# Expert weights of a mixture-of-experts layer: loads of 4 MB in four buffers instead of 2 MB in eight

## The chip, the core and the metric

The kernel runs on one core of a Trainium2 chip. The metric is the device time of one launch in microseconds. A TensorE matmul reads its weights (stationary operand) and its moving operand from SBUF and writes to PSUM; VectorE (DVE) and ScalarE (ACT) move and combine what it leaves there; the SyncE queue (SP) issues nearly all DMA transfers.

## What is computed

One decoder layer on 256 tokens of 1024 channels in float32: an input projection, a pooling mixer beside a dilated attention, an output projection, and then a mixture of experts, which is nearly all of the weight traffic:

```python
h2 = rmsnorm(x, g_ffn)
logits = h2 @ w_router + b_router            # 32 experts, the best 4 per token
for e in range(N_EXPERTS):
    gu = h2 @ w_gu[e] + b_gu[e]              # [256,1024] @ [1024,2048]
    gate = min(gu[:, :1024], 7);  lin = clip(gu[:, 1024:], -7, 7)
    act = gate * sigmoid(1.702 * gate) * (lin + 1)
    out += combine[:, e:e+1] * (act @ w_down[e] + b_down[e])     # [1024,1024]
return rmsnorm(x + out, g_final)
```

The weights of one expert are 8 MB of w_gu and 4 MB of w_down; all 32 experts are 384 MB (402.65 million bytes). Every expert is loaded, whichever tokens chose it.

## The kernel before

**Front part.** The first 120 us are the projections, the attention and the router. The input weights `win`, their split copies `wsp`, `hTh` and the output weights `wout` lie in the same 128 KB per partition of SBUF that later hold the expert weights (`raw`, line 105). So the first expert loads wait, one buffer after the other, until that part of the memory is free (lines 305 to 316).

**Units and buffers.** `raw` has eight buffers of 16 KB per partition, 2 MB each. A unit is one transfer into one buffer. A unit of w_gu is 256 rows of the matrix, two neighbouring rows to a partition; four units make an expert's w_gu. A unit of w_down is 512 rows, four neighbouring rows to a partition; two units make an expert's w_down. A partition's share is one contiguous run of 16 KB in memory either way (`load`, line 293). Because neighbouring rows lie in one partition, the other operand has to be taken with the same stride: `gather` takes the channels of `h2` with a step of two, `turn_gu` the columns of `gu` with a step of four, and the transposes of the bias (line 995) as well.

**Order.** Experts go in pairs. Up to 64 tokens are gathered for each (`gather`, with a one-hot matrix `disp` as moving operand); `gu_unit` multiplies one row of a w_gu unit per call, 16 matmul records per unit; ScalarE copies the sum from PSUM to `gu`; `turn_gu` transposes it; VectorE adds the bias and clips (`clip`), ScalarE takes the sigmoid, and VectorE forms `actT` (line 769). `down_unit` multiplies a w_down unit by it, 16 matmul records; ScalarE copies the result to `ysc`, and `scatter` multiplies it by the gates and adds it over the tokens. The second expert of a pair is worked on while the first one's activation is made: TensorE's order within `iteration` (line 1071) is w_gu of the pair's second expert (with the scatters of the pair before between its rows), w_down first half of the first expert, gathers for the next pair, `turn_gu`, w_down second half, w_gu of the next pair's first expert, then w_down of the second expert. The loads have the same order. The last pair has no next one.

**Release.** `unit_used` counts the units that TensorE has read. SP waits for the count that frees the buffer (line 335) and issues the next load into it. `raw_loaded[s]` says that buffer s has landed; TensorE waits for it at a unit's first matmul. All eight buffers (16 MB) are filled before the first expert's matmuls; the other 184 units follow one release after the other.

**End.** After the last w_down units come the last scatters, the sums, the final norm and two stores.

Of the kernel before, what the change touches and what calls it, by code (L numbers as in the profile page):

```python
# [42 lines left out]
UW = 2048  # L43
RAW = 8
GU_U, DN_U = 4, 2
EARLY = RAW - GU_U
# [38 lines left out]
def hybrid_layer(nc, x, g_mix, w_in, w_pool, pool_scale, w_out, g_ffn, w_router, b_router,  # L85
                 w_gu, b_gu, w_down, b_down, g_final, consts, out):
    KB = 1024
    with ExitStack() as ctx:
# [15 lines left out]
        W = PAD + T  # L104
        raw = at("raw", [P, RAW, 2, UW], F32, 0)
        acc = at("acc", [P, TT, D], F32, 144 * KB)
# [113 lines left out]
        x_loaded = [sem(f"x_loaded{t}") for t in range(TT)]  # L220
        raw_loaded = [sem(f"raw_loaded{s}") for s in range(RAW)]
        win_loaded = [sem(f"win_loaded{c}") for c in range(DC)]
        const_loaded, vec_loaded, wout_loaded = sem("const_loaded"), sem("vec_loaded"), sem("wout_loaded")
# [58 lines left out]
        def _(sp):  # L282
# [10 lines left out]
            def load(e, first, s):  # L293

                dst = raw[:, s].rearrange("p r n -> p (r n)")
                if first < GU_U:
                    src = w_gu[0, bass.ds(e, 1), 2 * first * P:2 * (first + 1) * P, :].rearrange(
                        "a (p r) n -> p (a r n)", r=2)
                else:
                    u = first - GU_U  # L300
                    src = w_down[0, bass.ds(e, 1), 4 * u * P:4 * (u + 1) * P, :].rearrange(
                        "a (p r) n -> p (a r n)", r=4)
                sp.dma_start(dst, src).then_inc(raw_loaded[s], 16)

            for c in range(PRE_U):
                sp.wait_ge(win_low, 2 * c + 2)
                load(0, c, c)
            sp.wait_ge(win_used, DC)
            load(1, 1, 5)
            load(1, 2, 6)  # L310
            sp.wait_ge(scores, 2)
            load(1, 0, 4)
            sp.wait_ge(probs_turned, 6)
            sp.dma_start(gffn[:], g_ffn.broadcast_to([P, D])).then_inc(gffn_loaded, 16)
            sp.wait_ge(half_projected, 1)
            load(1, 3, 7)
            sp.wait_ge(attended, 2)
# [9 lines left out]
            def iteration(j, half, last):  # L327
                i = j * 2 + half
                a = pair_of(i) * 2
                nxt = pair_of(i + 1) * 2  # L330
                for k in range(EARLY, ITER_U + (0 if last else EARLY)):
                    if last and k in range(GU_U + DN_U, 2 * GU_U + DN_U):
                        continue
                    at_ = k - (GU_U if last and k >= 2 * GU_U + DN_U else 0)
                    sp.wait_ge(unit_used, i * ITER_U + PRE_U + at_ - RAW + 1)
                    s = buffer(half, at_)
                    if k < GU_U + DN_U:
                        load(a, k, s)
                    elif k < 2 * GU_U + DN_U:
                        load(nxt, k - GU_U - DN_U, s)  # L340
                    elif k < ITER_U:
                        load(a + 1, k - GU_U - DN_U, s)
                    else:
                        load(nxt + 1, k - ITER_U, s)
# [56 lines left out]
        def _(act):  # L401
# [124 lines left out]
            def iteration(i, last):  # L526
                gu_copy(i * 2 + 1, 1, used(i, GU_U))
                if not last:
                    gather_copy(0, i * 2 + 3)
                    gather_copy(1, i * 2 + 4)  # L530
                sigmoid(i * 2 + 1)
                y_copy(i, 0, used(i, 6))
                if not last:
                    gu_copy(i * 2 + 2, 0, used(i, 10))
                    sigmoid(i * 2 + 2)
                    y_copy(i, 1, used(i, 12))
                else:
                    act.activation(scrap[:], c_("ones")[:, 0:1], ACT.Sqrt)
                    act.wait_ge(unit_used, used(i, ITER_U - GU_U))
                    act.activation(ysc[0:SLOTS, 1, :], ps[0:SLOTS, Y[1], :], ACT.Copy).then_inc(outputs_ready, 1)  # L540
# [281 lines left out]
        def _(pe):  # L822
# [169 lines left out]
            for m in range(DC):  # L992
                for h in range(2):
                    col = 2 * m + h
                    src = bgu[:, h * FE:(h + 1) * FE].rearrange("e (u q r) -> e u r q", q=P, r=4)[:, m // 4, m % 4, :]
                    ins = pe.transpose(ps[:, 2, col * E:(col + 1) * E], src, c_("ident", E)[:, 0:E])
# [13 lines left out]
            def gather(job):  # L1010

                for c in range(4 * job, 4 * job + 4):
                    for t in range(TT):
                        ins = mm(ps[:, M[job], (c % 4) * P:(c % 4 + 1) * P],
                                 h2[:, t, :].rearrange("p (k q r) -> p k r q", q=P, r=2)[:, c // 2, c % 2, :],
                                 disp[:, t, :, :], start=t == 0, stop=t == TT - 1)
                ins.then_inc(gathered, 1)

            def gu_unit(half, c, s, value):
                r = c % 2  # L1020
                if r == 0:
                    pe.wait_ge(raw_loaded[s], value)
                for b in range(2):
                    for h in range(2):
                        col = h * FE + b * 512
                        ins = mm(ps[h * SLOTS:(h + 1) * SLOTS, GU[half] + b, :], xT[:, c, half, :],
                                 raw[:, s, r, col:col + 512], start=c == 0, stop=c == DC - 1)
                if r == 1:
                    ins.then_inc(unit_used, 1)

            def down_unit(half, u, s, value):
                pe.wait_ge(raw_loaded[s], value)
                for r in range(4):
                    m = 4 * u + r
                    for h in range(2):
                        col = r % 2 * D + h * 512
                        ins = mm(ps[h * SLOTS:(h + 1) * SLOTS, Y[half], :], actT[:, half, m, :],
                                 raw[:, s, r // 2, col:col + 512], start=m == 0, stop=m == DC - 1)
                ins.then_inc(unit_used, 1)

            def turn_gu(e):

                pe.wait_ge(gu_copied, e + 1)
                for m in range(DC):
                    ins = pe.transpose(ps[:, M[m // 4], (m % 4) * P:(m % 4 + 1) * P],  # L1045
                                       gu[:].rearrange("p (u q r) -> p u r q", q=P, r=4)[:, m // 4, m % 4, :], c_("ident"))
                ins.then_inc(gu_turned, 1)
# [12 lines left out]
            for c in range(DC):  # L1060
                pe.wait_ge(xT_ready, c // 4 + 1)
                gu_unit(0, c, c // 2, 16)
            pe.wait_ge(bdown_loaded, 32)
# [7 lines left out]
            def iteration(j, half, last):  # L1071
                i = j * 2 + half
                for k in range(DC):
                    gu_unit(1, k, *unit(j, half, k // 2))
                    if k == 1:
# [17 lines left out]
                pe.wait_ge(act_ready, i * 2 + 1)  # L1093
                down_unit(0, 0, *unit(j, half, 4))
                if not last:
# [9 lines left out]
                turn_gu(i * 2 + 1)  # L1105
                down_unit(0, 1, *unit(j, half, 5))

                gap = GU_U if last else 0
                if not last:
                    for k in range(DC):  # L1110
                        gu_unit(0, k, *unit(j, half, 6 + k // 2))

                pe.wait_ge(act_ready, i * 2 + 2)
                for u in range(DN_U):
                    down_unit(1, u, *unit(j, half, 10 + u - gap))
                    if u == 0 and not last:
# [43 lines left out]
```

## Time and profile before

| | us |
|---|---|
| median of 3 runs | 1057.15 (1057.02 to 1059.78) |
| the profiled execution | 1058.68 |
| its span | 1056.9 |
| TensorE busy in it | 966.2 (91%) |
| VectorE, ScalarE busy | 248.6, 141.8 |
| transfers | 419.96 MB, mean 397 GB/s |

The page cuts the span into 40 slices of 26.4 us. A digit is the busy share in tenths, and PEclk the granted TensorE clock in tenths of full speed. The chain of waits is followed back from the last instruction, each step to what released it. In lists of instructions, x is the count, and the bracket is the idle time before and what ended it. MB and GB in the views are of 10^6 and 10^9 bytes, KB of 1024.

### The profile page before, as it was taken

What the parts mean: (1) busy time and instruction counts of PE and PEld (TensorE: products, weight loads), DVE (VectorE), ACT (ScalarE), POOL (GpSimd) and SP (SyncE); (2) the same over time, 40 slices, a digit from 0 to 9 for tenths busy, and PEclk for the clock granted to TensorE, in tenths of its full rate; (3) what the DMA queues carried; (4) which work ended last, traced back from release to release, by engine and by line L of the source; (5) the groups of instructions that cost most, each with busy time, mean ns of one, the idle gap of its engine ahead of it and who ended that gap; (6) DMA issues with size and microseconds to landing.
All of it is one profiled execution on the core that took longest, in us unless ns stands there. A gap on an engine that the chain in (4) does not pass through costs nothing.

```text
span 1056.9 us, 11867 instructions
## 1 busy us (share of the span) xinstructions
PE 966.2 (91%) x4791; PEld 421.7 (40%) x4791; DVE 248.6 (24%) x482; ACT 141.8 (13%) x213; POOL 12.8 (1%) x20
## 2 busy tenths in 40 slices
PE   6979999999999998999899998989999998989995
PEld 4956634343434342433334342423324342424331
DVE  4352521222222121212131211211131312212113
ACT  4340311010101010010101010100001010100102
POOL 0030000000000000000000000000000000000000
PEclk9999899999999999999999999999999999999998
DMA  9983099999999999999999999999999999999993
GB/s 377 408 324 110 26 376 422 425 428 428 427 428 429 427 431 427 428 428 428 428 429 428 427 430 428 430 428 427 430 427 430 428 428 428 428 429 428 427 427 148
DMA packets 32761, 419.96 MB, mean 397 GB/s; under 512 B 4596, under 2 KB 5128, under 8 KB 7112
## 3 DMA queue, kind: packets, MB, share of 16 engines
q1 hardware_dynamic: 32704, 419.71, 94.1%
q8 instruction: 13, 0.21, 0.1%
q14 instruction: 4, 0.03, 0.0%
q10 hardware_dynamic: 40, 0.01, 0.0%
HBM read 418.66 MB, written 1.05 MB: 397 GB/s over the span
## 4 chain that ended last, share of the span: by engine, by line
PE 52%; DMA 43%; DVE 2%; ACT 2%; issue 1%; SPq 0%; ACTq 0%; DVEq 0%
PE ps L824 49%; DMA raw<-in_w_down 39%; DMA raw<-in_w_gu 3%; PE ps L1045 2%; ACT xT L495 1%; DMA cst<-in_consts 1%; ACT pr L444 0%; PE ps L1089 0%; PE ps L931 0%; DVE sm L608 0%; DVE mxs L613 0%; DVE wsp L585 0%; ACT junk L412 0%; DVE outs L815 0%; ACT wsp L421 0%
## 5 line engine op out<-in xcount | busy, mean ns | idle before, releaser
L824 PE MATMUL ps<-raw,xT 128*64 128x512 f32 x2048 | 458.6, 596 | 23.9 <-DMA raw<-in_w_gu 23.9
L824 PEld LDWEIGHTS ps<-raw,xT 128*64 128x64 f32 x2048 | 140.6, 137 | 321.8 <-issue 262.3
L824 PE MATMUL ps<-raw,actT 128*64 128x512 f32 x1024 | 233.4, 597 | 25.1 <-DMA raw<-in_w_down 25.1
L759 DVE TENSOR_TENSOR biased<-ps,biasT 128x1024 f32<-128x1024 f32 x32 | 39.2, 1225 | 555.0 <-PE ps L1045 555.0
L824 PEld LDWEIGHTS ps<-raw,actT 128*64 128x64 f32 x1024 | 72.2, 136 | 161.9 <-issue 147.3
L502 ACT ACTIVATE gu<-ps 128x1024 f32<-128x1024 f32 x32 | 32.7, 1023 | 525.9 <-PE ps L824 525.9
L776 DVE TENSOR_TENSOR acc<-ps,acc 128x512 f32<-128x512 f32 x64 | 41.2, 685 | 133.9 <-PE ps L824 133.9
L824 PE MATMUL ps<-ysc,dispT 64*128 64x512 f32 x272 | 67.8, 615 | 0.8 <-DVE ysc L806 0.8
L824 PEld LDWEIGHTS ps<-disp,h 128*128 128x128 f32 x512 | 63.3, 201 | 12.9 <-issue 12.2
L824 PE MATMUL ps<-disp,h 128*128 128x128 f32 x512 | 66.4, 290 | 0.3 <-DVE disp L720 0.3
L1045 PE MATMUL ps<-cst,gu 128*128 128x128 f32 x256 | 39.4, 297 | 12.7 <-ACT xT L495 11.4
L1045 PEld LDWEIGHTS ps<-cst,gu 128*128 128x128 f32 x256 | 33.4, 210 | 29.3 <-issue 29.3
L824 PEld LDWEIGHTS ps<-ysc,dispT 64*128 64x128 f32 x272 | 24.0, 186 | 44.0 <-issue 29.4
L507 ACT ACTIVATE sig<-gate 128x512 f32<-128x512 f32 x32 | 20.2, 631 | 155.2 <-DVE gate L762 155.2
L824 PE MATMUL ps<-hTh,wsp 128*128 128x256 f32 x192 | 35.9, 283 | 1.6 <-DVE hTl L592 1.6
L824 PE MATMUL ps<-wout,mixT 128*128 128x512 f32 x64 | 30.2, 621 | 3.4 <-ACT mixT L454 3.4
L495 ACT ACTIVATE xT<-ps 128x512 f32<-128x512 f32 x32 | 19.1, 597 | 104.6 <-PE ps L824 104.6
L824 PEld LDWEIGHTS ps<-hTh,wsp 128*128 128x128 f32 x192 | 30.5, 192 | 2.1 <-DVE hTl L592 1.8
L824 PE MATMUL ps<-hTl,wsp 128*128 128x256 f32 x96 | 27.2, 283 | 0.0
L767 DVE TENSOR_TENSOR sig<-gate,sig 128x512 f32<-128x512 f32 x32 | 22.2, 693 | 11.6 <-ACT sig L507 11.6
L512 ACT ACTIVATE ysc<-ps 128x512 f32<-128x512 f32 x31 | 18.5, 597 | 36.5 <-PE ps L824 36.5
L585 DVE TENSOR_TENSOR wsp<-win,wsp 128x2048 fp32r<-128x2048 f32 x8 | 18.3, 2290 | 20.9 <-ACT wsp L421 20.9
(141 smaller groups left out, 335.7 us busy)
## 6 DMA issues: line engine op xcount, KB each, us to landing
raw<-in_w_gu SPq DMA_DIRECT2D x128, 2048.0 KB, 32.6
raw<-in_w_down SPq DMA_DIRECT2D x64, 2048.0 KB, 34.8
win<-in_w_in SPq DMA_DIRECT2D x8, 1024.0 KB, 15.2
wout<-in_w_out SPq DMA_DIRECT2D x1, 4096.0 KB, 32.5
acc<-in_x SPq DMA_DIRECT2D x2, 512.0 KB, 3.8
out<-outs SPq DMA_DIRECT2D x2, 512.0 KB, 3.1
gffn<-in_g_ffn SPq DMA_DIRECT2D x1, 512.0 KB, 3.6
gfin<-in_g_final SPq DMA_DIRECT2D x1, 512.0 KB, 3.3
```

The source lines that it names most:

```text
L495: act.activation(xT[:, 4 * job:4 * job + 4].rearrange("p c e s -> p (c e s)"), ps[:, M[job], :], ACT.Copy).then_inc(xT_ready, 1)
L502: act.activation(gu[:], ps[:, GU[half]:GU[half] + 2, :].rearrange("p a b -> p (a b)"), ACT.Copy).then_inc(gu_copied, 1)
L507: act.activation(sig[:], gate[:], ACT.Sigmoid, scale=ALPHA).then_inc(sig_done, 1)
L512: act.activation(ysc[:, half, :], ps[:, Y[half], :], ACT.Copy).then_inc(outputs_ready, 1)
L585: dve.tensor_tensor(wsp[c % 2][:, 1, :], win[:, c, :], wsp[c % 2][:, 0, :].bitcast(F32), ALU.subtract).then_inc(win_low, 1)
L759: dve.tensor_tensor(biased[:].rearrange("p m x s -> p (m x) s"), turned, bc(biasT[:, :, bass.ds(e, 1)], P, 2 * DC, SLOTS), ALU.add).then_i ...
L767: dve.tensor_tensor(sig[:], gate[:], sig[:], ALU.mult).then_inc(gsig_done, 1)
L776: dve.tensor_tensor(part, ps[:, M[job % 2], :], part, ALU.add).then_inc(added, 1)
L824: return pe.matmul(out_, lhsT, rhs, start=start, stop=stop, skip_group_check=shared)
L1045: ins = pe.transpose(ps[:, M[m // 4], (m % 4) * P:(m % 4 + 1) * P], gu[:].rearrange("p (u q r) -> p u r q", q=P, r=4)[:, m // 4, m % 4, :] ...
```

## The change

The same bytes go through the same 128 KB per partition in half as many pieces. `raw` becomes four buffers of 32 KB per partition. A w_gu transfer holds four neighbouring rows per partition (two transfers to an expert), a w_down transfer the whole matrix, eight rows per partition. The strides of `h2`, `gu` and `b_gu` become four, eight and eight. `unit_used` is raised once per 4 MB. Only the very last w_down matrix is loaded in two transfers of 2 MB with semaphores of their own (`load_last`). The first fills of the buffers are issued under the waits that free all of a larger buffer. Everything else keeps its order.

```diff
 UW = 2048
-RAW = 8
-GU_U, DN_U = 4, 2
+RAW = 4
+ROWS = 4
+GU_U, DN_U = 2, 1
...
-        raw = at("raw", [P, RAW, 2, UW], F32, 0)
+        raw = at("raw", [P, RAW, ROWS, UW], F32, 0)
...
                 if first < GU_U:
-                    src = w_gu[0, bass.ds(e, 1), 2 * first * P:2 * (first + 1) * P, :].rearrange(
-                        "a (p r) n -> p (a r n)", r=2)
+                    src = w_gu[0, bass.ds(e, 1), ROWS * first * P:ROWS * (first + 1) * P, :].rearrange(
+                        "a (p r) n -> p (a r n)", r=ROWS)
                 else:
-                    u = first - GU_U
-                    src = w_down[0, bass.ds(e, 1), 4 * u * P:4 * (u + 1) * P, :].rearrange(
-                        "a (p r) n -> p (a r n)", r=4)
+                    src = w_down[0, bass.ds(e, 1), :, :].rearrange("a (p r) n -> p (a r n)", r=2 * ROWS)
                 sp.dma_start(dst, src).then_inc(raw_loaded[s], 16)
 
+            def load_last(e, s):
+
+                for u in range(2):
+                    src = w_down[0, bass.ds(e, 1), :, :].rearrange("a (p r) n -> p (a r) n", r=2 * ROWS)[:, 4 * u:4 * u + 4, :]
+                    dst = raw[:, s, 2 * u:2 * u + 2].rearrange("p r (b n) -> p (r b) n", b=2)
+                    sp.dma_start(dst, src).then_inc(tail_loaded[u], 16)
+
             for c in range(PRE_U):
-                sp.wait_ge(win_low, 2 * c + 2)
+                sp.wait_ge(win_low, ROWS * c + ROWS)
                 load(0, c, c)
             sp.wait_ge(win_used, DC)
-            load(1, 1, 5)
-            load(1, 2, 6)
             sp.wait_ge(scores, 2)
-            load(1, 0, 4)
+            load(1, 0, 2)
             sp.wait_ge(probs_turned, 6)
             sp.dma_start(gffn[:], g_ffn.broadcast_to([P, D])).then_inc(gffn_loaded, 16)
             sp.wait_ge(half_projected, 1)
-            load(1, 3, 7)
+            load(1, 1, 3)
...
-                    src = bgu[:, h * FE:(h + 1) * FE].rearrange("e (u q r) -> e u r q", q=P, r=4)[:, m // 4, m % 4, :]
+                    src = bgu[:, h * FE:(h + 1) * FE].rearrange("e (q r) -> e r q", r=DC)[:, m, :]
...
-                                 h2[:, t, :].rearrange("p (k q r) -> p k r q", q=P, r=2)[:, c // 2, c % 2, :],
+                                 h2[:, t, :].rearrange("p (k q r) -> p k r q", q=P, r=ROWS)[:, c // ROWS, c % ROWS, :],
...
-                r = c % 2
+                r = c % ROWS
                 if r == 0:
                     pe.wait_ge(raw_loaded[s], value)
...
-                if r == 1:
+                if r == ROWS - 1:
                     ins.then_inc(unit_used, 1)
...
-            def down_unit(half, u, s, value):
-                pe.wait_ge(raw_loaded[s], value)
-                for r in range(4):
-                    m = 4 * u + r
+            def down_part(half, u, s, value, last=False):
+                if last:
+                    pe.wait_ge(tail_loaded[u], 16)
+                elif u == 0:
+                    pe.wait_ge(raw_loaded[s], value)
+                for m in range(4 * u, 4 * u + 4):
                     for h in range(2):
-                        col = r % 2 * D + h * 512
+                        col = m % 2 * D + h * 512
                         ins = mm(ps[h * SLOTS:(h + 1) * SLOTS, Y[half], :], actT[:, half, m, :],
-                                 raw[:, s, r // 2, col:col + 512], start=m == 0, stop=m == DC - 1)
-                ins.then_inc(unit_used, 1)
+                                 raw[:, s, m // 2, col:col + 512], start=m == 0, stop=m == DC - 1)
+                if u == 1:
+                    ins.then_inc(unit_used, 1)
...
-                                       gu[:].rearrange("p (u q r) -> p u r q", q=P, r=4)[:, m // 4, m % 4, :], c_("ident"))
+                                       gu[:].rearrange("p (q r) -> p r q", r=DC)[:, m, :], c_("ident"))
```

## Rows read from the trace of the kernel before

**Rows 1.** The page: three of the lines of 40 slices.

```profile
PE   6979999999999998999899998989999998989995
DMA  9983099999999999999999999999999999999993
GB/s 377 408 324 110 26 376 422 425 428 428 427 428 429 427 431 427 428 428 428 428 429 428 427 430 428 430 428 427 430 427 430 428 428 428 428 429 428 427 427 148
```

**Rows 2.** The page: the chain that ended last, by line.

```profile
PE ps L824 49%; DMA raw<-in_w_down 39%; DMA raw<-in_w_gu 3%; PE ps L1045 2%; ACT xT L495 1%; DMA cst<-in_consts 1%; ACT pr L444 0%; PE ps L1089 0%; PE ps L931 0%; DVE sm L608 0%; DVE mxs L613 0%; DVE wsp L585 0%; ACT junk L412 0%; DVE outs L815 0%; ACT wsp L421 0%
```

**Rows 3.** That chain in order of time: start us, us, what.

```profile
348.81 30.45 DMA raw<-in_w_down
...
999.71 35.30 DMA raw<-in_w_down
1035.15 9.18 PE ps L824 x40
```

**Rows 4.** Waits of TensorE: total us, times, longest us.

```profile
PE ps L824 <- DMA raw<-in_w_down: 25.1, 24, 1.3
PE ps L824 <- DMA raw<-in_w_gu: 23.9, 22, 1.2
```

**Rows 5.** Transfers from 500 to 900 us (packets of 16 KB).

```profile
DMA packets 11769, 171.43 MB, mean 429 GB/s; under 512 B 1306, under 2 KB 1306, under 8 KB 1306
```

**Rows 6.** Transfers from 11 to 22 us (8 KB) and from 28 to 34 us (4 KB).

```profile
DMA packets 652, 4.70 MB, mean 428 GB/s; under 512 B 78, under 2 KB 78, under 8 KB 78
...
DMA packets 613, 2.46 MB, mean 410 GB/s; under 512 B 2, under 2 KB 14, under 8 KB 613
```

**Rows 7.** SP's DMA issues: start us, us to the last one's end, line, tensors, count.

```profile
61.90 3.24 SPq L303 DMA_DIRECT2D raw<-in_w_gu  x3
98.01 0.33 SPq L303 DMA_DIRECT2D raw<-in_w_gu  x1
98.38 0.43 SPq L318 DMA_DIRECT2D bgu<-in_b_gu  x1
133.53 3.70 SPq L303 DMA_DIRECT2D raw<-in_w_down  x2
149.74 7.92 SPq L303 DMA_DIRECT2D raw<-in_w_gu  x2
164.93 0.33 SPq L303 DMA_DIRECT2D raw<-in_w_down  x1
177.94 4.13 SPq L303 DMA_DIRECT2D raw<-in_w_gu  x2
```

**Rows 8.** Stretch 134 to 136 us: length, busy times, clock, DMA share, GB/s.

```profile
134.00:136.00 2.00, 2.00 (x12) 0.67 (x10) 0.00 (x0) 0.00 (x0) 0.00 (x0) 1.00 0.83 164
```

**Rows 9.** Instructions of TensorE in order of time, from 115 to 200 us.

```profile
118.39 2.10 PE L996 MATMUL ps<-cst,bgu 32*128 32x32 f32 x16
129.61 13.96 PE L824 MATMUL ps<-raw,xT 128*64 128x512 f32 x64
145.91 3.65 PE L824 MATMUL ps<-raw,xT 128*64 128x512 f32 x16
199.47 3.60 PE L824 MATMUL ps<-raw,xT 128*64 128x512 f32 x16
```

**Rows 10.** The same, near the end.

```profile
1025.37 3.65 PE L824 MATMUL ps<-raw,actT 128*64 128x512 f32 x16 [0.82 <-DMA raw<-in_w_down]
1028.95 1.23 PE L1045 MATMUL ps<-cst,gu 128*128 128x128 f32 x8
```

**Rows 11.** VectorE, near the end.

```profile
1033.34 0.69 DVE L769 SCALAR_TENSOR_TENSOR actT<-lin,sig 128x512 f32<-128x512 f32 x1
```

**Rows 12.** Groups of weight loads: busy us, mean ns of one, idle us before.

```profile
L824 PEld LDWEIGHTS ps<-disp,h 128*128 128x128 f32 x512 | 63.3, 201 | 12.9 <-issue 12.2 <-DVE disp L720 0.7
L1045 PEld LDWEIGHTS ps<-cst,gu 128*128 128x128 f32 x256 | 33.4, 210 | 29.3 <-issue 29.3
L1089 PEld LDWEIGHTS ps<-cst,gated 128*128 128x128 f32 x64 | 6.7, 141 | 13.0 <-issue 6.5 <-DVE acc L776 6.5
```

More of the change, by code:

```diff
@@ L221, in hybrid_layer @@
         raw_loaded = [sem(f"raw_loaded{s}") for s in range(RAW)]
+        tail_loaded = [sem(f"tail_loaded{u}") for u in range(2)]
         win_loaded = [sem(f"win_loaded{c}") for c in range(DC)]
@@ L340, in iteration @@
                         load(nxt, k - GU_U - DN_U, s)
+                    elif last:
+                        load_last(a + 1, s)
                     elif k < ITER_U:
@@ L531, in iteration @@
                 sigmoid(i * 2 + 1)
-                y_copy(i, 0, used(i, 6))
+                y_copy(i, 0, used(i, GU_U + DN_U))
                 if not last:
-                    gu_copy(i * 2 + 2, 0, used(i, 10))
+                    gu_copy(i * 2 + 2, 0, used(i, 2 * GU_U + DN_U))
                     sigmoid(i * 2 + 2)
-                    y_copy(i, 1, used(i, 12))
+                    y_copy(i, 1, used(i, ITER_U))
                 else:
@@ L1061, in _ @@
                 pe.wait_ge(xT_ready, c // 4 + 1)
-                gu_unit(0, c, c // 2, 16)
+                gu_unit(0, c, c // ROWS, 16)
             pe.wait_ge(bdown_loaded, 32)
@@ L1073, in iteration @@
                 for k in range(DC):
-                    gu_unit(1, k, *unit(j, half, k // 2))
+                    gu_unit(1, k, *unit(j, half, k // ROWS))
                     if k == 1:
@@ L1093, in iteration @@
                 pe.wait_ge(act_ready, i * 2 + 1)
-                down_unit(0, 0, *unit(j, half, 4))
+                down_part(0, 0, *unit(j, half, GU_U))
                 if not last:
@@ L1105, in iteration @@
                 turn_gu(i * 2 + 1)
-                down_unit(0, 1, *unit(j, half, 5))
+                down_part(0, 1, *unit(j, half, GU_U))
                 gap = GU_U if last else 0
@@ L1110, in iteration @@
                     for k in range(DC):
-                        gu_unit(0, k, *unit(j, half, 6 + k // 2))
+                        gu_unit(0, k, *unit(j, half, GU_U + DN_U + k // ROWS))
                 pe.wait_ge(act_ready, i * 2 + 2)
-                for u in range(DN_U):
-                    down_unit(1, u, *unit(j, half, 10 + u - gap))
+                for u in range(2):
+                    down_part(1, u, *unit(j, half, 2 * GU_U + DN_U - gap), last)
                     if u == 0 and not last:
```

## The prediction

> **What bounds the kernel now.** I read the forty slices of the page first [rows 1]. From slice 6 on the DMA digit is 9 and the rate stands at 422 to 431 GB/s until the last slice. TensorE shows 9 in the early slices and 8 to 9 later, so it is close behind. In slices 4 and 5 the rate falls to 110 and 26 GB/s: there all sixteen megabytes of weight buffers are full and nothing has been used yet. The chain that ended last [rows 2] is TensorE for 49%, then transfers of w_down for 39%; its last pieces [rows 3] are a transfer from 999.71 to 1035.01 and TensorE behind it. TensorE's waits on raw are 46, none over 1.3 us, evenly on both weight tensors [rows 4]: it catches each unit as it lands. So two limits follow one another. The first uses of the buffers run ahead of the loads (the work on one expert pair takes TensorE 53.6 us early on, 145.91 to 199.47 [rows 9], and its twelve transfers 58.7), the reserve is eaten by about 350 us, where the chain first goes through a transfer [rows 3], and from there each unit is waited for. What sets the end is therefore the transfer stream: the time of its first packet, its rate, any holes in it, and TensorE's work after the last landings. TensorE's own speed in the middle changes nothing.
>
> The stream's numbers: 171.43 MB in 400 us is 428.6 GB/s [rows 5], so a unit of 2048 KB (2.097 MB) takes 4.893 us. The first refill is issued at 133.53 [rows 7]; the stretch from 134 to 136 moves 164 GB/s [rows 8], which is 0.77 us at the full rate, so the first packet is at about 135.2, 1.7 us behind its issue. 184 of the 192 units are loaded in this stream, 900 us of it.
>
> **Part 1: a buffer is given back only after 4 MB.** TensorE starts on the first weights at 129.61 and takes 13.96 us for the first four old units [rows 9], 3.44 us from one start to the next. SP issued at 133.53 after one unit; now it needs two, 136.97. The stream starts 3.44 us later, and nothing hides that, because the stream has no hole later in which to catch up: +3.4 us.
>
> Holes in the new stream, with 9.71 us a load (part 2), the releases being those of every second unit in SP's queue [rows 7]: first data 138.7; load 1 (issued near 143.8, after the fourth old unit) follows at once and ends at 158.1. Load 2 is released when both halves of its buffer are read, at 157.33 (149.74 plus 7.92 less 0.33 of the issue), with data at 159.0: a hole of 0.9. Load 3 (164.93) is in time and ends at 178.5. Load 4 now waits for the whole down projection of the first expert, in whose middle the gathers and transposes stand: 177.94, data at 179.6, a hole of 1.2. After it TensorE releases faster than the loads run and there are no more. The old stream by the same working has one hole of 0.4 at that place. Net +1.7 us. Behind these 0.9 and 1.2 stands the assumption that a queue with less than 1.7 us of work left runs dry; at the least they are nothing, at the most the full 1.7 each (3.4), so this term is between 0 and +3.
>
> In the middle no load is late: when TensorE waits for one buffer, the two or three behind it are already queued, 20 to 29 us of work.
>
> **Part 2: rows of 32 KB.** No packet of more than 16 KB is in this trace. Three stretches give the price of smaller ones: 601 packets of 4 KB in 6 us (613 less 12 small ones, 410 GB/s) are 159.8 ns a packet and engine; 574 of 8 KB in 11 us (652 less 78, 428 GB/s) are 306 ns [rows 6]; 10463 of 16 KB in 400 us (11769 less 1306 small ones) are 611.7 ns [rows 5]. From 4 and 16 KB: 150.6 ns per 4 KB and 9.2 ns fixed. From 8 and 16 KB: next to nothing fixed, 0.7 ns. The stretches of the small packets are short, and an error of 1% in the 306 moves that result by 6 ns, so I take the pair with the wide distance. A packet of 32 KB is then 1214 ns, a load of 4 MB (eight packets an engine) 9.71 us in place of 9.787: 0.074 us. 91 loads stand in the stream before the last full one lands: -6.7 us. Bounds: no gain (rows cut at 16 KB, or 8 against 16 KB believed); at best the whole fixed part goes, 91 loads of 16 x 9.2 ns, -13.4 us. A loss is possible too, since no row shows such a length (last rival).
>
> The number of transfers halves as well. That is nothing by itself: their issues (0.33 us each on SP) lie beside a stream that never waits for them in the middle. Here a rule would say more. The Trainium skill, "SBUF — State Buffer", section "The DMA setup-cost knee", gives a fixed cost of roughly 2 us for every transfer and advises the largest transfers. By that rule 91 transfers fewer would be 182 us less. The trace speaks against it: 4.893 us for 2.097 MB leaves no room for 2 us in each, since seven transfers are queued and the fixed parts overlap. The sum does without it.
>
> **Part 3: the tail.** Now the first half of the last w_down matrices no longer arrives before its second. The old landings are 4.89 us apart: the next to last unit at 1035.01 [rows 3], so the second half of the first expert's down weights at 1030.1 and the first half at 1025.2; TensorE starts them at 1025.37 [rows 10]. From 1030.1 to TensorE's end of down work at 1044.33 are 14.2 us. In the new kernel that matrix lands as one, at the time of its second half. Then follow: 0.14 to the first matmul, 3.58 for its first half (1025.37 to 1028.95), from the start of the transposes to actT finished 5.08 (1028.95 to 1034.03) [rows 10, 11], in which the second half (3.58) fits, 0.06 of start, and 9.18 for the last two halves and the scatters between them (1035.15 to 1044.33) [rows 3]. That is 18.0 us: +3.8. The last load stays cut in two; its halves land 4.9 and 9.8 us after that matrix and are wanted 8.9 and 14.4 us after it, so both are hidden with 4 us to spare. Its inner rows may become packets of 4 KB (159.8 ns against 153), some 0.2 us each, in that slack.
>
> **Part 4: strides.** The transposes of gu now read every eighth element, and the gathers every fourth. Weight loads of gu at stride four take 210 ns, of gated without stride 141, of h2 at stride two 201 [rows 12], yet eight transposes of gu take 1.23 us (0.13 apart) [rows 10] and that hides nearly all of it. The Trainium skill, "SBUF — State Buffer", names a line of 16 bytes in its text on SBUF "cachelines": a read that crosses to a new line each time pays. Stride four already does, so by it strides of eight cost no more; that is in line with 210 against 141 but no row shows eight. On the path lie two lots: the gathers before 129.61 and one turn in the tail. I take +0.3, bounds 0 and +1.5 (each of these operations at double distance).
>
> **Part 5: the start.** Loads into what is now buffer 2 move from the queue's 61.90 to after the scores (near 64.8), done by 76; those into buffer 3 to 98.01, 4 MB in place of 2, and push b_gu (98.38) back 4.9 us, from about 107.5 to 112.4 [rows 7]. TensorE turns b_gu at 118.39 [rows 9], so 6 us of cover remain; were it gone, each further us would be on the path. Nothing added.
>
> **Sum.** +3.4 + 1.7 - 6.7 + 3.8 + 0.3 = +2.5 us. Made against the profiled execution (span 1056.9, time 1058.7) it is a span of 1059.4 and a time of 1061.2; against the median 1057.15, 1.5 lower than the profiled one, 1059.7.
>
> **Rivals.** (a) *The long rows bring nothing*: packets stay 16 KB or their cost grows with bytes. For it: 428 GB/s at 8 KB and 428.6 at 16 KB. Against: 410 at 4 KB. The delays of parts 1, 3 and 4 (+9.2) remain uncovered: 1066.3, and it decides against "no change" as soon as part 2 gives less than 6 us. (b) *The fixed part goes further*: beyond the packets something of each transfer is saved, down to -13.4 in part 2, or the holes of part 1 do not open. 1057.15 + 9.2 - 13.4 = 1053.0. Against: the small packets of 4 bytes, one an engine and transfer, are the only thing of a transfer that the rows show. (c) *Long rows slow the memory*: each engine's reading point then moves in larger steps, and sixteen of them meet. Priced by the slowest unbroken rate in the trace, 410 GB/s, the 893 us of stream become 933: +40 on the 9.2, 1106; it wins from a rate of 427. The Trainium skill, "DMA: Bandwidth & Descriptors", section "Latency and other measured facts", reports half the rate at row pitches of megabytes; here w_out's rows, 4 KB pieces half a megabyte apart, still run at 410, so I hold it small.
>
> **How the numbers follow.** 0.3% of 1057 is 3.2 us, about what a measurement here can tell from no change: same is 1054.0 to 1060.3. My forecast (part 2 giving 5 to 8 us, so +1.2 to +4.2) has 0.58, of which 0.39 under +3.2 and 0.19 over; (a) with 0.24 is slower; (c) 0.05; (b) 0.13, of which 0.06 is still within 0.3%. Faster 0.07, same 0.45, slower 0.48. The likeliest case alone reaches from 1057.5 to 1062; the range takes in (a) to its end and half of (b): 1056 to 1066.5.
>
> **What the profile after would show.** First refill issued at 137.0; packets of 32 KB (half as many) and a rate of 431 to 432 GB/s in the middle, 428.6 if (a), less if (c); holes near 158 and 179; the first expert's last down matmuls starting 18 us before the end of the down work; b_gu's turn still at 118. I am wrong if the rate in the middle is above 434 or below 428, or if the last down matmuls wait for their own transfer rather than for actT.

## The result

The changed kernel takes 1065.83 us (median of 6 runs, 1064.63 to 1066.13) against 1058.93 for the kernel before, run beside it: a ratio of 1.0067, 95% interval 1.0056 to 1.0078, or 7 us slower. The profiled execution took 1066.07 with a span of 1064.3, 7.4 over that of before. The forecast was +2.5; the sign is as forecast, the time lies inside the range, but outside the likeliest case (+1.2 to +4.2), and it got there by another way than the rival that reaches so far.

The page of the changed kernel, to be held against [rows 1]. From slice 8 on the transfers are at 9 and 425 to 434 GB/s, but slices 6 and 7 (313, 338) are lower than before (376, 422), and TensorE now shows 9 nearly everywhere:

```profile
PE   6989999999999999999999999999999999999995
DMA  9873278999999999999999999999999999999992
GB/s 375 331 316 132 81 313 338 433 433 432 432 425 432 431 430 430 434 434 434 432 432 431 430 434 430 431 432 430 434 434 434 432 431 432 430 434 428 430 427 91
```

The chain that ended last, by line, against [rows 2]: w_down transfers were 39% of it and are 13%; TensorE's main line was 49% and is 77%. The chain first passes through a transfer of expert weights at 714 us, where it did at 349 before [rows 3].

```profile
PE ps L831 77%; DMA raw<-in_w_down 13%; PE ps L1055 3%; ACT xT L502 1%; PE ps L1099 1%; DMA cst<-in_consts 1%; PE ps L848 0%; ACT pr L451 0%; PE ps L938 0%; DVE sm L615 0%; DVE mxs L620 0%; ACT junk L419 0%; DVE outs L822 0%; PE ps L975 0%; DVE acc L818 0%
```

TensorE's waits for w_down (total us, times, longest us), against [rows 4]. With one of 0.2 us for w_gu they are six with 3.1 us, where there were 46 with 49.0 us.

```profile
PE ps L831 <- DMA raw<-in_w_down: 2.9, 5, 0.7
```

Transfers from 500 to 900 us, against [rows 5]. 5929 packets less 656 small ones are 5273 of 32 KB in 400 us over 16 engines: 1213.7 ns each, where I had worked out 1214. A 4 MB transfer takes 9.71 us.

```profile
DMA packets 5929, 172.79 MB, mean 432 GB/s; under 512 B 656, under 2 KB 656, under 8 KB 656
```

The groups of weight loads, against [rows 12]. The loads of h2 for the gathers (`disp,h`) went from 201 to 329 ns; those of gu, now at stride eight, from 210 to 196.

```profile
L831 PEld LDWEIGHTS ps<-disp,h 128*128 128x128 f32 x512 | 120.7, 329 | 12.9 <-issue 12.2
...
L1055 PEld LDWEIGHTS ps<-cst,gu 128*128 128x128 f32 x256 | 32.7, 196 | 29.3 <-issue 29.3
```

TensorE and SP's issues in order of time, against [rows 7, 9]. The first 32 gather matmuls take 7.73 us (5.86 before), the first expert matmul is at 131.90 (129.61), the first refill at 139.25 (133.53), the fifth at 183.78. The gathers of a pair take 7.73 in place of 4.04.

```profile
124.23 7.73 PE L831 MATMUL ps<-disp,h 128*128 128x128 f32 x32 [0.34 <-DVE disp L727]
131.90 13.96 PE L831 MATMUL ps<-raw,xT 128*64 128x512 f32 x64
...
170.36 7.73 PE L831 MATMUL ps<-disp,h 128*128 128x128 f32 x32
```

```profile
139.25 0.37 SPq L303 DMA_DIRECT2D raw<-in_w_down  x1
146.11 13.80 SPq L303 DMA_DIRECT2D raw<-in_w_gu  x2
167.19 0.33 SPq L303 DMA_DIRECT2D raw<-in_w_down  x1
183.78 7.19 SPq L303 DMA_DIRECT2D raw<-in_w_gu  x2
```

Stretches of the stream there (length, busy times, clock, DMA share, GB/s): a small hole after 160, a large one after 179, with nothing at all from 181 to 183. Against 432 GB/s the bytes that are missing are worth 0.7 us in the first and 5.0 us in the second (179 to 189). A packet of 1.2 us is counted as a whole in one stretch, so the edges are no sharper than that.

```profile
160.00:162.00 2.00, 2.00 (x10) 0.68 (x12) 1.99 (x9) 0.00 (x0) 0.00 (x0) 1.00 0.92 279
162.00:179.00 17.00, 16.24 (x73) 10.28 (x70) 0.35 (x3) 2.22 (x3) 0.00 (x0) 1.00 1.00 431
179.00:181.00 2.00, 2.00 (x14) 1.30 (x16) 0.77 (x1) 0.00 (x0) 0.00 (x0) 1.00 0.69 295
181.00:183.00 2.00, 2.00 (x13) 0.58 (x9) 1.60 (x4) 0.63 (x1) 0.00 (x0) 1.00 0.00 0
183.00:185.00 2.00, 2.00 (x12) 0.71 (x10) 1.00 (x2) 0.60 (x1) 0.00 (x0) 1.00 0.67 180
```

The end on TensorE, against [rows 10] and the last of [rows 3]. The first expert's down matmuls start behind their transfer at 1033.91; the second expert's wait for actT, not for their own transfer; the end is at 1042.55 plus 9.18, 1051.7, that is 18.0 us after the landing at 1033.77. Two pieces of the chain, then TensorE in order of time:

```profile
1006.43 27.34 DMA raw<-in_w_down
...
1042.55 9.18 PE ps L831 x40
```

```profile
1033.91 3.65 PE L831 MATMUL ps<-raw,actT 128*64 128x512 f32 x16 [0.67 <-DMA raw<-in_w_down]
1037.49 1.16 PE L1055 MATMUL ps<-cst,gu 128*128 128x128 f32 x8
1038.58 3.65 PE L831 MATMUL ps<-raw,actT 128*64 128x512 f32 x16
1042.55 3.65 PE L831 MATMUL ps<-raw,actT 128*64 128x512 f32 x16 [0.31 <-DVE actT L776]
```

### The profile page after: what moved, and what is told of

Its sections match the earlier page's. It is cut to its first block, busy times and chain, and to the rows that moved or that the text cites. A ratio compares the mean times of both kernels' runs of the same rounds, so it can differ in the third digit from the quotient of the medians.

```text
span 1064.3 us, 11511 instructions
## 1 busy us (share of the span) xinstructions
PE 1022.2 (96%) x4791; PEld 481.8 (45%) x4791; DVE 248.8 (23%) x482; ACT 142.2 (13%) x213; POOL 12.8 (1%) x20
## 4 chain that ended last, share of the span: by engine, by line
PE 82%; DMA 13%; DVE 2%; ACT 2%; issue 1%; ACTq 0%; SPq 0%; DVEq 0%
PE ps L831 77%; DMA raw<-in_w_down 13%; PE ps L1055 3%; ACT xT L502 1%; PE ps L1099 1%; DMA cst<-in_consts 1%; PE ps L848 0%; ACT pr L451 0%; PE ps L938 0%; DVE sm L615 0%; DVE mxs L620 0%; ACT junk L419 0%; DVE outs L822 0%; PE ps L975 0%; DVE acc L818 0%
## 5 line engine op out<-in xcount | busy, mean ns | idle before, releaser
L831 PE MATMUL ps<-raw,actT 128*64 128x512 f32 x1024 | 236.3, 604 | 3.3 <-DMA raw<-in_w_down 2.9
L831 PEld LDWEIGHTS ps<-disp,h 128*128 128x128 f32 x512 | 120.7, 329 | 12.9 <-issue 12.2
L831 PE MATMUL ps<-disp,h 128*128 128x128 f32 x512 | 123.7, 402 | 0.3 <-DVE disp L727 0.3
```

Source lines behind the costliest of these rows:

```text
L831: return pe.matmul(out_, lhsT, rhs, start=start, stop=stop, skip_group_check=shared)
```

## The experiments

The part before the first expert matmul differs by up to 4.5 us between profiled executions (that matmul is at 127.5 to 131.9), also where nothing in it was changed. So beside the medians I give the *expert stretch* of each profile: from TensorE's first expert matmul to the end of the down work. It is 914.7 us in the kernel before (129.61 to 1044.33) and 919.8 in the changed one; the first gathers lie ahead of it. The kernel before was timed beside each of them, with medians from 1058.6 to 1059.6; the ratios are to these.

**1. h2 in the order of the gathers.** My theory after the result was that the gathers' weight loads account for all that the forecast lacked. VectorE writes h2 so that each gather's weights lie side by side; the transfers stay as changed.

```diff
-                dve.scalar_tensor_tensor(out=h2[:, t, :], in0=acc[:, t, :], scalar=rs[:, t:t + 1], in1=gffn[:], ...
+                for k in range(DC // ROWS):
+                    lo, hi = k * ROWS * P, (k + 1) * ROWS * P
+                    ins = dve.scalar_tensor_tensor(out=h2[:, t, lo:hi].rearrange("p (r q) -> p q r", r=ROWS),
+                                                   in0=acc[:, t, lo:hi].rearrange("p (q r) -> p q r", r=ROWS), ...
...
-                                 h2[:, t, :].rearrange("p (k q r) -> p k r q", q=P, r=ROWS)[:, c // ROWS, c % ROWS, :],
+                                 h2[:, t, c * P:(c + 1) * P],
```

> The changed kernel with one edit: the normalised activations h2 are written to SBUF in the order in which the gathers read them, so that the gathers' weight loads have no stride. Theory (the 4.6 us above the forecast are the gathers, whose weight loads went from 201 to 329 ns, first in the start and then in a hole of the transfer stream): 32 gather matmuls take 4.0 us and not 7.7, the first refill is issued near 137.4 and not 139.25, the hole before the fifth refill shrinks from 5 us to about 1, the rate stays 432 GB/s; time 5 to 6 us under the changed kernel, 1060 to 1061. Rival (the holes come from the 4 MB transfers themselves, which start later behind an emptied queue): the hole stays near 5 us and the time falls by at most 2 us, 1064.

Measured: 1059.94 (11 runs), ratio to before 1.0011 (1.0002 to 1.0020), against 1.0067 of the changed kernel. The first refill is issued at 138.47, a microsecond later than expected. The fifth is issued at 179.11 and the stream falls to 295 and 311 GB/s there in place of stopping, a hole of 1.2 us; the rate stays 432. Expert stretch 915.7.

```profile
L837 PEld LDWEIGHTS ps<-disp,h 128*128 128x128 f32 x512 | 60.2, 197 | 12.9 <-issue 12.2 <-DVE disp L733 0.7
```

```profile
178.00:180.00 2.00, 2.00 (x12) 0.61 (x10) 1.32 (x2) 0.60 (x1) 0.00 (x0) 1.00 0.69 295
180.00:182.00 2.00, 2.00 (x12) 0.72 (x10) 0.00 (x0) 0.00 (x0) 0.00 (x0) 1.00 0.93 311
```

The theory holds in its size: 5.9 us come from one stride. The edit shortens two things at once, the hole and TensorE's work in every pair, so it doesn't tell them apart. It cost something on VectorE: four writes of 1.1 us (two of 1.28 before), some 0.9 us more on the way to the first gathers.

**2. The same stride alone, in the kernel before.**

```diff
-                                 h2[:, t, :].rearrange("p (k q r) -> p k r q", q=P, r=2)[:, c // 2, c % 2, :],
+                                 h2[:, t, :].rearrange("p (k q r) -> p k r q", q=P, r=4)[:, c // 4, c % 4, :],
```

> The kernel before with one edit: the gathers read h2 at a stride of four elements instead of two (they take other channels than the matrix needs, so the expert sums are others; the work is the same). Theory (strides alone cost it): gathers 7.7 us in place of 4.0, first refill near 135.4, one hole of 3 to 4 us where the tenth unit is refilled, rate unchanged 428.6 GB/s, time +5.5 us, 1064.4. Rival (TensorE has 5 us of slack a pair and hides it): only the first gather counts, +1.9 us, 1060.8.

Measured: 1065.63, ratio 1.0064 (1.0044 to 1.0085), +6.8 us. So a stride alone costs the old kernel about as much as the whole change does. A hole of some 4 us opens there too, where the old kernel only fell to about 400 GB/s (176 to 184):

```profile
180.00:182.00 2.00, 2.00 (x12) 0.61 (x10) 1.69 (x3) 0.58 (x1) 0.00 (x0) 1.00 0.43 180
182.00:184.00 2.00, 2.00 (x12) 0.72 (x10) 1.39 (x2) 0.65 (x2) 0.00 (x0) 1.00 0.02 8
184.00:186.00 2.00, 2.00 (x12) 0.67 (x10) 0.00 (x0) 0.00 (x0) 0.00 (x0) 1.00 0.94 229
```

It is 1.3 us more than I expected, and the way is not the one that I expected either. From the first gathers on, the chain that ended last is TensorE's: there is no transfer of expert weights in it, and TensorE waits for none of them, where it did 46 times before.

```profile
PE ps L824 89%; PE ps L1045 4%; PE ps L1089 1%; ACT xT L495 1%; DMA cst<-in_consts 1%; PE ps L841 0%; ACT pr L444 0%; PE ps L931 0%; DVE sm L608 0%; DVE mxs L613 0%; ACT junk L412 0%; DVE outs L815 0%; PE ps L968 0%; DVE acc L811 0%; ACT mi
```

```profile
349.00:354.00 5.00, 4.24 (x17) 2.40 (x18) 1.90 (x3) 0.81 (x2) 0.00 (x0) 0.66 1.02 433
```

The first line is the chain by line, the second a stretch as above. So the hole is there but doesn't set the end; TensorE's own work does. TensorE is slower by 3.7 us in each pair, which uses up nearly all of the 5.1 us that a pair of transfers left it (58.7 against 53.6). The granted clock takes the rest: in the second line it is 0.66 of full speed, a mean between the levels of 1.2 and 2.4 GHz, and the eight transposes of gu and the w_down unit behind them take 1.98 and 4.38 us there, against 1.24 and 3.65 at full clock in the same pair. Without such a place two pairs take 114.4 us (179.48 to 293.90), with one 115.9 to 116.0, six times in a row up to 989.69: some 9 us. The expert stretch is 920.2, 5.5 over before. The transfers alone would have made it some 3 us longer, by my estimate from the time of their last packets.

**3. What a stride costs, by itself.**

> No expert layer at all: only TensorE, 32 float32 matmuls of 128x128 at each stride of the weights' columns (1, 2, 4, 8 elements; tiles by_0 to by_3) and 32 transposes each of the same (tiles turned_0 to turned_3). The output is not the layer's. Theory (a stride of four elements and more costs, whatever the tensor): weight loads of by_0 and by_1 about 195 ns, by_2 and by_3 about 330; for the transposes 141 to 210 ns at all strides, as the traces of both kernels show. Rival (it is h2's place in SBUF or the transfers beside it that slow its loads): by_2 and by_3 stay near 200.

Measured, weight loads in a stretch of each kind; by line 140 for matmuls at strides 1, 2, 4 and 8 in this order:

```profile
L140 PEld LDWEIGHTS ps<-cst,by 128*128 128x128 f32 x55 | 6.2, 192 | 0.0
L140 PEld LDWEIGHTS ps<-cst,by 128*128 128x128 f32 x53 | 6.3, 196 | 0.0
L140 PEld LDWEIGHTS ps<-cst,by 128*128 128x128 f32 x53 | 12.5, 329 | 0.0
L140 PEld LDWEIGHTS ps<-cst,by 128*128 128x128 f32 x56 | 13.4, 335 | 0.0
```

TensorE in order of time, the 64 matmul records of each stride and 32 transposes behind them:

```profile
57.02 7.31 PE L140 MATMUL ps<-cst,by 128*128 128x128 f32 x64
64.17 3.66 PE L144 MATMUL ps<-cst,turned 128*128 128x128 f32 x32
67.66 7.70 PE L140 MATMUL ps<-cst,by 128*128 128x128 f32 x64
75.20 3.99 PE L144 MATMUL ps<-cst,turned 128*128 128x128 f32 x32
79.03 15.09 PE L140 MATMUL ps<-cst,by 128*128 128x128 f32 x64
93.95 3.99 PE L144 MATMUL ps<-cst,turned 128*128 128x128 f32 x32
97.78 15.39 PE L140 MATMUL ps<-cst,by 128*128 128x128 f32 x64
113.00 3.71 PE L144 MATMUL ps<-cst,turned 128*128 128x128 f32 x32
```

For matmuls a step of two elements is nearly free, a step of four halves the speed, eight is 2% slower than four. Transposes load in 140, 209, 209 and 191 ns, and 32 of them take 3.66, 3.99, 3.99 and 3.71 us: they don't have that step. Hardly a transfer runs beside it (at most 4 GB/s in the stretches of matmuls looked at) and the tiles lie elsewhere, so the rival falls.

**4. The coarse grain alone**, with 2 MB transfers and rows of 16 KB.

```diff
-                    sp.wait_ge(unit_used, i * ITER_U + PRE_U + at_ - RAW + 1)
+                    sp.wait_ge(unit_used, i * ITER_U + PRE_U + at_ - RAW + 1 + (1 - at_ % 2))
...
+                if c % 4 == 0:
+                    pe.wait_ge(raw_loaded[s + 1], value)
...
+                if u == 0 and not last:
+                    pe.wait_ge(raw_loaded[s + 1], value)
```

> The kernel before, still with 2 MB transfers and rows of 16 KB, but SP refills a buffer only when both of a pair are read and TensorE starts a pair only when both have landed (all but the last w_down pair, as in the change). This is the coarse grain alone. Theory: first refill near 137.0, holes of together about 1.5 us, and 18 us from the landing of the last pair's first w_down matrix to the end of the down work instead of 14.2; rate 428.6 GB/s; +8.5 us, 1067. Rival (the grain costs only the late start, the rest is hidden): +3.4, 1062.3.

Measured: 1067.46, ratio 1.0084 (1.0067 to 1.0101), +8.4 to 8.9. Expert stretch 922.6, +7.9. The first refill is 7.35 us behind the first expert matmul and the tail 18.0 us, as in the changed kernel. The grain costs what parts 1 and 3 of the prediction said (+8.9), and the rate is unchanged (428 GB/s).

**5. Only the release coarse** (the first line of the diff above, without the two waits).

> The kernel before with only the release made coarse: SP refills a 2 MB buffer when both of its pair are read; TensorE waits for each unit by itself. Theory: the late start and the holes are from the release (about +5), the tail from the landing (+3.4), so this gives 1064, between the kernel before and the pairs of 2 MB (1067.5). Rival: the landing alone makes the tail and the release costs only what the first refill is late, 1062.4.

Measured: 1062.73, ratio 1.0039 (1.0024 to 1.0053), +4. Expert stretch 918.4: +3.7 for the release and 4.2 more for the landing by pairs (922.6). The first refill is 7.35 us behind the first expert matmul here too. The landing's part is about as foreseen (3.8); that of the release is 1.4 under my 5.1. The median lies nearer to the rival (1062.4), yet a hole is there (340 GB/s from 176 to 180), so I take the split between late start and holes as uncertain to about a microsecond.

**6. 4 MB transfers with rows of 16 KB.** Each partition gets two runs of 16 KB from the old places, in one transfer.

```diff
-                    src = w_gu[0, bass.ds(e, 1), ROWS * first * P:ROWS * (first + 1) * P, :].rearrange(
-                        "a (p r) n -> p (a r n)", r=ROWS)
+                    src = w_gu[0, bass.ds(e, 1), ROWS * first * P:ROWS * (first + 1) * P, :].rearrange(
+                        "a (b p r) n -> p (a b) (r n)", b=2, r=2)
...
```

> The changed kernel with its 4 MB transfers, four buffers and releases, but each partition's share comes as two runs of 16 KB from the places of the kernel before, so the strides of h2, gu and b_gu are two and four again. Theory (the gain in rate belongs to the length of a row, not to the size of a transfer): rate 428.6 to 429 GB/s, 9.78 us a transfer, gathers 4.0 us, time as the pairs of 2 MB, about 1067. Rival (it belongs to the size of a transfer): 432 GB/s, 9.71 us, about 1060.5.

Measured: 1066.57, ratio 1.0079 (1.0062 to 1.0095). 11116 packets less 656 small ones are 10460 of 16 KB in 400 us, 611.9 ns each as before; the small ones halved and brought nothing that shows.

```profile
DMA packets 11116, 171.38 MB, mean 428 GB/s; under 512 B 656, under 2 KB 656, under 8 KB 656
```

The gain in rate belongs to the row length. Halving the number of transfers without it gains nothing: 611.9 ns a packet against 611.7 before.

**7. Fine grain where it is on the path.** If the price of the grain is paid at the two ends only, and the gain in rate all along, then cutting a few transfers in two should keep the gain and drop the price. With h2 in order, the six refills of the first pair are released, loaded and waited for by halves of 2 MB, and so are the last four loads before the tail.

```diff
+                    if k in halves:
+                        ...
+                        if start:
+                            sp.wait_ge(half_used, PRE_U + at_ - RAW + 1)
+                            load_half(e, first, s, 0)
+                        sp.wait_ge(unit_used, i * ITER_U + PRE_U + at_ - RAW + 1)
+                        if not start:
+                            load_half(e, first, s, 0)
+                        load_half(e, first, s, 1)
+                        continue
...
-            with sp.Fori(0, last_two) as j:
+            iteration(0, 0, False, range(2, 8), True)
+            iteration(0, 1, False)
+            with sp.Fori(1, last_two) as j:
```

> h2 in the gathers' order, as in the first experiment, and the 4 MB transfers cut into two halves of 2 MB only where the coarse grain was on the path: the six refills of the first pair of experts, released and waited for by halves, and the last four before the tail. The other 81 transfers keep rows of 32 KB. Theory (start, holes and tail are the price of the grain, and the gain in rate is independent of them): first refill 3.4 us earlier than in the first experiment, no hole over 0.5 us until 230, about 14 us or less from the landing of the first expert's last w_down to the end of the down work, 432 GB/s in the middle; 1053 to 1055, that is 4 to 6 us under the kernel before. Rival (the time lost at the ends comes back elsewhere, TensorE being close behind the transfers): 1058 to 1060, as the first experiment.

Measured: 1051.57, ratio 0.9933 (0.9917 to 0.9948): 7.8 us faster than the kernel before, and 1.4 below the range expected. The rate is 432, the stream runs at 401 to 442 GB/s through 176 to 190, and SP's first refills (3.7 us behind the first expert matmul at 128.23) and TensorE's end are as fine as in the kernel before: the second expert's down matmuls wait for their own transfer again.

```profile
131.93 3.76 SPq L316 DMA_DIRECT2D raw<-in_w_down  x2
138.80 17.27 SPq L316 DMA_DIRECT2D raw<-in_w_gu  x4
```

```profile
1018.13 3.65 PE L863 MATMUL ps<-raw,actT 128*64 128x512 f32 x16 [1.18 <-DMA raw<-in_w_down]
...
1027.78 3.65 PE L863 MATMUL ps<-raw,actT 128*64 128x512 f32 x16 [1.32 <-DMA raw<-in_w_down]
```

**8. Each end by itself.** The same kernel without the early halves, and without the late ones.

> As the kernel with halves at both ends, but without the early ones: only the last four w_gu and w_down transfers before the tail are cut in two. Theory (each end has its own price): the holes and the late first refill stay, from the landing of the second half of the first expert's last w_down to the end of the down work 14 to 15 us in place of 18; 3 to 4 us under the kernel with h2 in order, 1056 to 1057. Rival (the tail is TensorE's own work and hides the landings): no more than 1 us under it, 1059.

> As the kernel with halves at both ends, but without the late ones: only the six refills of the first pair of experts are released, loaded and waited for by halves. Theory: the first refill 3.4 us earlier against TensorE's first expert matmul, no hole near 180 us, tail as in the changed kernel (18 us); 4.5 to 5.5 us under the kernel with h2 in order, 1054.5 to 1055.5. Rival (TensorE is the bound by then and an earlier stream gains nothing): 1059.

Measured: late only 1058.34, ratio 1.0001 (0.9991 to 1.0011); early only 1057.19, ratio 0.9987 (0.9978 to 0.9996). Against h2 in order (1.0011) these are 1.1 and 2.5 us, together less than half of the 8 that both gave. Both expectations of a gain were too high. The expert stretches say otherwise: 913.9 and 911.8 against 915.7, and 908.7 with both: 1.8, 3.9 and 7.0. Since the medians of both ends, of each end and of h2 in order were taken on three different chips, each beside the kernel before, two of the kernels were timed again side by side.

> The kernel with halves at both ends again, now in one job with the early-only kernel, since the three medians did not add up (late only -1, early only -2.5, both -8 against h2 in order) while the traces nearly do (-1.8, -3.9, -7.0 from TensorE's first expert matmul to the end of the down work). If the traces are right: 3 us under the early-only kernel of the same job and 5 to 6 under the kernel before, 1053 to 1054. If the two ends help each other: 5.5 under it, 1051.5.

> The early-only kernel again in the same job. If the traces are right 1055 to 1056.5, 2.5 to 3.5 us under the kernel before; if the first medians are, 1057, 1.5 under it.

Measured: both ends 1053.57, ratio 0.9948 (0.9934 to 0.9962); early only 1056.91, ratio 0.9978 (0.9969 to 0.9987), 2.3 to 2.7 us under the kernel before: nearer to the case of the traces (2.5 to 3.5) than to that of the first medians (1.5), though just above the range of times given for it. The late halves are worth 3.3 us beside the early ones, as the traces had it (3.1 then; now stretches of 908.8 and 912.2). The kernel with both is 5.5 to 7.8 us faster than the kernel before, the first chip having shown more. Why the late halves gain 3.3 on top of the early ones and only 1 to 2 alone stays open in part. The traces show where the difference is: in the late-only kernel the second half of the matrix lands at about 1030.7, 899.7 us into the stretch, where with h2 in order it lands 897.8 in, so 1.9 of the tail's 3.8 us are lost in the stream. Beside the early halves the same landing is later by only 0.3 to 0.6 us (893.9 and 894.3 in early only, 894.5 and 894.6 with both, reckoned back from the last landing). Four loads with rows of 16 KB cost 0.3, by the prices of the packets. What else held the stream up in the late-only kernel isn't shown.

## Why the prediction was right or wrong

| step | predicted, us | measured, us |
|---|---|---|
| first refill after TensorE's first expert matmul | +3.4 | 7.35 in place of 3.92: +3.4 |
| holes | +1.7 | 0.7 and 5.0, less the old 0.4: +5.3 |
| rows of 32 KB | -6.7 | 9.71 a transfer in place of 9.787: -7.0 |
| tail | +3.8 | 18.0 in place of 14.2: +3.8 |
| strides | +0.3 | +1.9 ahead of the first expert matmul (and 3.6 of the holes, counted above) |
| front part | 0 | +0.4, no more than its spread |
| sum | +2.5 | +7.8 worked out, +7.4 in the spans |

**What held.** The bound, though only just (the stream sets the end, with TensorE much closer behind than before), the late start, the price of a 32 KB packet, worked out from packets of 4 and 16 KB to within a nanosecond, and the tail, step by step. Experiment 6 confirms that the gain is the row's and not the transfer's, as part 2 put it, and so that the setup rule of the Trainium skill ("SBUF — State Buffer", "The DMA setup-cost knee") has nothing to give in a queue that is never empty. b_gu's transposes stood at 118.80 and waited for nothing, as foreseen. Two slips changed nothing: 574 packets of 8 KB in 11 us are 306.6 ns and not 306, which leaves 1.5 ns fixed between 8 and 16 KB and not 0.7; and in [rows 1] the rate is 376 GB/s in slice 6 and 422 only from slice 7 on.

**The step that failed is part 4.** The change raises two strides, and I priced both by one row: the loads of gu at stride four, 210 ns. That row is of transposes. The gathers are plain matmuls, for which the trace of before had only stride two, 201 ns; for them four is the step from 196 to 329. My upper bound of 1.5 us was also no bound: 32 gather matmuls at double distance are 4 us more, and they come in every pair. The Trainium skill had the rule in the paragraph that I used ("SBUF — State Buffer", the text on SBUF "cachelines"): a 16-byte line should be hit at least twice. Two float32 elements of a line are read at stride two and one at stride four. I checked gu by it, which already had one, and not h2, which lost its second. Experiment 3 agrees with the rule for matmul weights (192, 196, 329, 335 ns) and not for transposes, and it disagrees with the page's figure that a stride of four float32 elements is free.

**Then the cover.** I had written that TensorE's own speed in the middle changes nothing. In the changed kernel that is barely so: a pair takes TensorE 57.1 us (in the chain from 180.01 to 237.06; its gathers went from 4.04 to 7.73) against 58.3 of transfers (six of 9.71), and TensorE waits for weights six times, 3.1 us in all. In experiment 2 it is not so: TensorE's own work sets the end. And before the slack is used up, the gathers do harm at one place. They stand between the two halves of the w_down matrix whose release the fifth load waits for, so this load is issued 51.9 us behind the first expert matmul in place of 48.3: 3.7 us of TensorE became 3.6 us of hole. With the hole the matrix of the tail lands 901.9 us into the stretch, and 897.8 in experiment 1: 4.1 us, all of the difference between their stretches. But both edits change the hole and TensorE's work together. No run closes the hole alone, and with 3.1 us of waits left TensorE would soon have set the end instead. So it is shown that the stride costs the 6 us, and not how they divide between the two. TensorE time is free only as long as a pair's work stays below its transfers, and where no release that the stream is waiting for hangs behind it.

**The range** held the result by luck, because of rival (a), whose mechanism did not occur: the long rows gave all they promised. It was right for the wrong reason. The chances leaned the right way (slower 0.48), half of that through (a); the likeliest case, +1.2 to +4.2, did not come.

## What to carry to other kernels

In this stream of queued transfers a longer row saved a small fixed time per packet (9 to 10 ns of 612), and fewer transfers saved nothing; the coarser grain that comes with it cost time at the two ends, where a buffer's first release and last landing are on the path. Keep the long rows in the middle and cut only the transfers at the ends. And when a layout change alters an operand's stride, price every reader of it separately, by the kind of instruction: a float32 matmul's weights went from 196 to 329 ns between steps of two and four elements, a transpose's stayed at 209. Then hold the slower engine's whole work against the slack that it had, and not only its work on the path.

## What the runs showed of the hardware that I had not expected

- A float32 matmul's weights at a stride of four elements load in 329 ns against 196 at two, and the matmuls follow at 0.24 us apart against 0.12; a transpose's don't differ (209 at both).
- The granted TensorE clock dips in the changed kernel where it doesn't before: mean 0.68 of full speed from 292 to 296 us, and 0.83 from 980 to 990, that is between the levels of 1.2 and 2.4 GHz. In the stretch before the first (286 to 292) TensorE was busy all the time with gathers, whose weight loads filled it. The eight transposes of gu at 986.41 took 1.97 us instead of 1.16. After both places TensorE still waited for transfers, so no cost at the end is seen; in experiment 2, where it waited for none, such places cost some 9 us. The slow gathers aren't needed for them: with h2 in order the mean is 0.91 from 350 to 360 us, behind a stretch in which TensorE was busy all the time and its weight loads a third of it.

```profile
286.00:290.00 4.00, 4.00 (x19) 4.00 (x18) 0.00 (x0) 0.60 (x1) 0.00 (x0) 1.00 1.06 459
290.00:292.00 2.00, 2.00 (x10) 2.00 (x9) 0.00 (x0) 0.00 (x0) 0.00 (x0) 1.00 0.91 393
292.00:296.00 4.00, 3.24 (x13) 1.81 (x15) 1.16 (x1) 0.60 (x1) 0.00 (x0) 0.68 1.05 451
```
